# Where the gate rows of a two-mixer transformer step are computed, and in which order its first loads go out

## Chip, core and metric

One NeuronCore of a Trainium2 chip runs the whole program. The time is device microseconds (us) of one execution. An execution taken by the hardware profiler has two times: the time of that execution, and its span, from the first to the last instruction of the profile.

## What is computed

One inference step of a layer with two groups of heads, all in float32. 128 context tokens and 512 latent tokens (five token tiles of 128) have 2048 features each. Cut to what matters here:

```
mod                = silu(cond) @ w_ada + b_ada       # 2 conditionings (latent, context), w_ada 2048 x 6144
shift, scale, gate = split(mod, 3)                    # each 2 rows of 2048
h  = rms_norm(x, g_norm) * (1 + scale) + shift
z  = h @ w_in                                         # mixer A: 8 heads; mixer B: 8 heads, 2 KV heads
oa = differential attention of mixer A (softmax 1 - lambda * softmax 2), RMS norm, times silu(ga)
ob = grouped-query attention of mixer B with RMS norm on q and k, times silu(gb)
y  = rms_norm(x + gate * (concat(oa, ob) @ w_out), g_final)
```

Shift and scale are needed before any token is projected. The gate rows are needed only at the end, when the output projection is added to x. The keys and values of the context tokens are outputs too.

## The kernel before

**Passes.** The projections run as 17 passes (`ITS`) of 16 steps (`KT`, one per 128 features of the contraction). Every step multiplies five token tiles by one 128x512 block of weights into the PSUM tile `z_ps`. Each factor is split into a high and a low float32r part, so a tile costs three matmuls of 512 columns (L542, L543, L544), 15 in a step. Pass 0 (`KV_IT`) makes the keys and values of mixer B, passes 1 to 4 (`G_IT`) two query heads of mixer B each with their gates, passes 5 to 12 (`D_IT` to `OUT_IT - 1`) one head of mixer A each, and passes 13 to 16 the output projection, 512 columns each.

**Attention beside the projection.** While pass `it` is projected, TensorE does the attention of the group of pass `it - 1` between the token tiles, by the table `STEPS`: O (output rows of the group before) in step 1, QK (transposes of q and k) in step 3, then S (scores), T (transposes of the probabilities) and V (times the values) of tile after tile, with T of the last tile in step 14 and V of the last tile, called V4 below, in step 15, after the second token tile. ScalarE and VectorE each run one hand-ordered list per step: the split of the weights three steps ahead (`split_w`: ScalarE copies `w_raw` to `w_hi` at L794, VectorE subtracts at L1100), the evictions, maxima (L1180), exponentials, the subtraction of the softmaxes (L1197), the split of the transposed probabilities (`pt_los`, L1205), `v_lo`, `qk_los` (L1171), norms and rotary positions (`rotate`, L1129 to L1143). GpSimd takes reciprocal roots (`o_root`), the products with the gates (`gate_mul`) and a queue of DMAs of its own (`load_kv`, `state`, `spill`, `load_row`, `load_out_operands`). All other loads are on SyncE's queue. The three banks of `ring` (PSUM) are handed out by `count_turns`; a bank is claimed again when its last reader has freed it.

**Pass 0 and the start.** The shift and scale columns of w_ada (32 MB) come in 32 loads `load_ada(n)` of 1 MB (two DMAs of 512 KB) into a ring of five (`ADA_RING`). Each is one quarter of a block of two feature tiles, multiplied by the two conditioning columns (`modulation`, L562, 32 matmul instructions with two stationary columns). Four quarters are a block; VectorE takes its rows from PSUM (L1052), TensorE transposes them (`columns`, L575), and only then can two more feature tiles of h be scaled (`modulate`, L815 and L819) and split (`split_h`, L1092 and L1094). The work on block c+1 and c+2 stands between the token tiles of pass 0; the last quarter, (7, 3), is in step 12. SyncE issues four w_ada loads, the five tiles of x (1 MB each), load 4, the first two pairs of weight steps (`load_w`), and then the rest. ScalarE squares each x tile (L804), GpSimd takes the root, VectorE scales it (L1074), TensorE transposes it (L585). GpSimd's queue begins with the small tables: four broadcasts of 256 KB for lambda, three of 64 KB for norm weights, and the two rotary tables. VectorE uses the lambda tables in step 3 of pass 0 (`minus_lambda`).

**Gate rows.** The gate columns of w_ada (16 MB) come in 32 loads of 512 KB (`load_gate`, L494) on SyncE's queue into eight buffers that lie in attention tiles not yet used. TensorE multiplies them by the two conditioning columns (`step_gate`, L744) after 18 steps: 13, 14 and 15 of pass 0 and 0 to 14 of pass 1, one or two loads each, always into bank 0 of the ring. A load is two products of 128x2 stationary and 128x512 moving, whose outputs go to partitions 0, 32, 64 or 96, each of which runs as two matmul instructions. `gate_rows_out` (L1260, four additions on VectorE) adds the bias at the start of pass 2, and `norm_sums` and `gate_exp` of pass 1's group wait for the last gate product, since their tiles overlay the buffers. GpSimd loads the bias in pass 1 and writes the rows to DRAM in pass 2.

```
    take("GATE", [0])                                             # L170
            if it == G_IT + 1 and s == 0: gate_rows_out()         # L1363
STEPS = { 1: O, 3: QK, 4: S0, 5: S1, 6: T0, 7: S2 V0, 8: T1, 9: S3 V1, 10: T2, 11: S4 V2, 12: T3, 13: V3, 14: T4, 15: V4 }
```

## Time and profile before

| | |
|---|---|
| median of 3 runs | 1334.58 us (1333.96 to 1335.18) |
| the profiled execution | 1334.56 us |
| its span | 1332.8 us |
| TensorE busy | 1277.5 us, 96% of the span |
| VectorE, ScalarE, GpSimd busy | 719.2, 606.9, 216.7 us |
| DMA | 156.59 MB, mean 117 GB/s; 301 to 359 GB/s in the first four fortieths of the span |
| granted TensorE clock | 0.998 of full speed |

Busy times are of instructions on an engine. Matmuls are pipelined, so a row's duration is longer than the distance between two starts; where a length of TensorE work is wanted, starts are to be compared. A DMA's time to landing counts from its issue.

### The profile page before, as it was taken

What the parts mean: (1) busy time and instruction counts of PE and PEld (TensorE: products, weight loads), DVE (VectorE), ACT (ScalarE), POOL (GpSimd) and SP (SyncE); (2) the same over time, 40 slices, a digit from 0 to 9 for tenths busy, and PEclk for the clock granted to TensorE, in tenths of its full rate; (3) what the DMA queues carried; (4) which work ended last, traced back from release to release, by engine and by line L of the source; (5) the groups of instructions that cost most, each with busy time, mean ns of one, the idle gap of its engine ahead of it and who ended that gap; (6) DMA issues with size and microseconds to landing.
All of it is one profiled execution on the core that took longest, in us unless ns stands there. A gap on an engine that the chain in (4) does not pass through costs nothing.

```text
span 1332.8 us, 19103 instructions
## 1 busy us (share of the span) xinstructions
PE 1277.5 (96%) x7399; PEld 1009.7 (76%) x7399; DVE 719.2 (54%) x1155; ACT 606.9 (46%) x1297; POOL 216.7 (16%) x374
## 2 busy tenths in 40 slices
PE   2699999999999999999999999999999999999996
PEld 1466666788888888877778787878788787888885
DVE  1443531856647566465565656565656766523343
ACT  1322312454555545545554645555555665422123
POOL 2000110301103011021212222121213222200001
PEclk9999999999999999999999999999999999999999
DMA  9999784211212112131222121221213431433234
GB/s 301 359 353 347 273 275 142 64 48 48 69 47 83 48 48 76 52 92 48 82 65 77 59 78 56 68 81 49 85 48 108 124 107 64 138 132 134 79 135 158
DMA packets 144218, 156.59 MB, mean 117 GB/s; under 512 B 8008, under 2 KB 122792, under 8 KB 143360
## 3 DMA queue, kind: packets, MB, share of 16 engines
q1 hardware_dynamic: 137232, 132.19, 30.7%
q0 software_dynamic: 6896, 23.17, 5.3%
q8 instruction: 59, 0.97, 0.3%
q14 instruction: 31, 0.25, 0.1%
HBM read 144.18 MB, written 11.16 MB: 117 GB/s over the span
## 4 chain that ended last, share of the span: by engine, by line
PE 89%; DVE 3%; DMA 3%; SPq 2%; ACT 1%; issue 1%; POOL 0%; ACTq 0%; DVEq 0%
PE z_ps L542 24%; PE z_ps L544 22%; PE z_ps L543 22%; PE ring L637 5%; PE ring L718 5%; PE ring L673 4%; PE ring L720 2%; PE ring L562 2%; SPq L455 1%; DMA x_sb<-in_x_sample_dram 1%; PE ring L744 1%; PE ring L544 1%; PE ring L543 1%; PE ring L542 1%; DMA ada_raw<-in_w_ada_dram 1%; DMA w_raw<-in_w_in_dram 1%
## 5 line engine op out<-in xcount | busy, mean ns | idle before, releaser
L542 PE MATMUL z_ps<-w_hi,xt_hi 128*128 128x512 f32 x1360 | 570.6, 420 | 2.4 <-DVE xt_lo L1244 1.0
L544 PE MATMUL z_ps<-w_hi,xt_lo 128*128 128x512 f32 x1360 | 532.7, 392 | 0.0
L543 PE MATMUL z_ps<-w_lo,xt_hi 128*128 128x512 f32 x1360 | 532.1, 391 | 0.0
L1100 DVE TENSOR_TENSOR w_lo<-w_raw,w_hi 128x512 fp32r<-128x512 f32 x272 | 191.6, 707 | 247.7 <-ACT w_hi L794 245.7
L794 ACT ACTIVATE w_hi<-w_raw 128x512 fp32r<-128x512 f32 x272 | 170.4, 628 | 334.0 <-PE z_ps L544 321.6
L542 PEld LDWEIGHTS z_ps<-w_hi,xt_hi 128*128 128x128 f32 x1360 | 256.1, 188 | 80.5 <-issue 35.5
L544 PEld LDWEIGHTS z_ps<-w_hi,xt_lo 128*128 128x128 f32 x1360 | 255.6, 188 | 56.7
L543 PEld LDWEIGHTS z_ps<-w_lo,xt_hi 128*128 128x128 f32 x1360 | 257.3, 189 | 36.2
L1180 DVE TENSOR_REDUCE small<-s_sb 128x2 f32<-128x1536 f32 (+1 forms) x60 | 88.3, 1472 | 29.2 <-ACT s_sb L794 29.2
L896 ACT ACTIVATE s_sb<-s_sb,small 128x768 f32<-128x768 f32 (+1 forms) x120 | 97.9, 819 | 2.8 <-DVE small L1180 2.8
L718 PE MATMUL ring<-v_hl,pt_hi 128*128 128x256 f32 x400 | 96.2, 324 | 0.0
L794 ACT ACTIVATE o_sum<-ring 128x128 f32<-128x128 f32 (+1 forms) x60 | 18.8, 313 | 159.9 <-PE ring L720 159.9
L720 PE MATMUL ring<-v_hl,pt_lo 128*128 128x128 f32 x400 | 89.0, 223 | 0.0
L1205 DVE TENSOR_TENSOR pt_lo<-ring,pt_hi 128x256 fp32r<-128x256 f32 (+2 forms) x144 | 75.2, 527 | 24.4 <-ACT pt_hi L794 21.4
L794 ACT ACTIVATE pt_hi<-ring 128x256 fp32r<-128x256 f32 (+2 forms) x144 | 66.7, 467 | 47.0 <-PE ring L637 45.9
L1448 POOL TENSOR_TENSOR sg<-sg,zs 128x128 f32<-128x128 f32 (+1 forms) x60 | 37.0, 616 | 290.8 <-DVE sg L1163 290.1
L720 PEld LDWEIGHTS ring<-v_hl,pt_lo 128*128 128x128 f32 x400 | 76.3, 191 | 3.1
L718 PEld LDWEIGHTS ring<-v_hl,pt_hi 128*128 128x128 f32 x400 | 75.2, 188 | 3.2
L1163 DVE RECIPROCAL sg<-sg 128x128 f32<-128x128 f32 (+1 forms) x60 | 72.6, 1209 | 3.4 <-POOL sg L1442 3.4
L794 ACT ACTIVATE s_sb<-ring 128x512 f32<-128x512 f32 (+2 forms) x144 | 59.4, 464 | 29.0 <-PE ring L673 28.2
L637 PE MATMUL ring<-ident,s_sb 128*128 128x128 f32 x400 | 66.4, 272 | 0.0
L1216 DVE TENSOR_TENSOR o_sum<-ring,o_sum 128x128 f32<-128x128 f32 (+1 forms) x60 | 20.0, 334 | 84.8 <-ACT o_sum L794 84.8
(147 smaller groups left out, 1199.4 us busy)
## 6 DMA issues: line engine op xcount, KB each, us to landing
w_raw<-in_w_in_dram SPq DMA_DIRECT2D x208, 256.0 KB, 3.2
ada_raw<-in_w_ada_dram SPq DMA_DIRECT2D x64, 512.0 KB, 8.8
w_raw<-in_w_out_dram SPq DMA_DIRECT2D x64, 256.0 KB, 3.4
gate_pt<-in_w_ada_dram SPq DMA_DIRECT2D x12, 512.0 KB, 6.2
gate_sg<-in_w_ada_dram SPq DMA_DIRECT2D x12, 512.0 KB, 5.4
o_spill<-row_st POOLq DMA_DIRECT2D x14, 320.0 KB, 3.5
row_st<-o_spill POOLq DMA_DIRECT2D x14, 320.0 KB, 3.4
x_sb<-in_x_sample_dram SPq DMA_DIRECT2D x4, 1024.0 KB, 13.7
```

Source lines behind the costliest of these rows:

```text
L542: pe.matmul(out, hi_l, hi_r, start=start, stop=False)
L543: pe.matmul(out, hi_l, lo_r, start=False, stop=False)
L544: return pe.matmul(out, lo_l, hi_r, start=False, stop=stop)
L637: return pe.transpose(bank[:, col:col + P], src, ident[:, :])
L718: pe.matmul(bank[:, o:o + 2 * DH], pt_hi[:, c_, keys], v_hl[:, vh, vt, :], start=(j == 0), stop=False, skip_group_check=True)
L720: ins = pe.matmul(bank[:, o:o + DH], pt_lo[:, c_, keys], v_hl[:, vh, vt, 0:DH], start=False, stop=(j == tiles[-1][0]), skip_group_check=True)
L794: return act.activation(out, in_, ACT.Copy, **kw)
L896: act.activation(row, row, ACT.Exp, bias=nmax[:, t, c_:c_ + 1], accum_out=den[:, t, c_:c_ + 1]).then_inc(exp_done, 1)
L1100: dve.tensor_tensor(w_lo[:, b, :], w_raw[:, kg // 2 % RAW_RING, kg % 2, :], w_hi[:, b, :].bitcast(F32), ALU.subtract).then_inc(w_lo_done, 1)
L1163: dve.reciprocal(sg[:, t, 0:w], sg[:, t, 0:w]).then_inc(g_inv, 1)
L1180: dve.tensor_reduce(nmax[:, t, :], s_sb[:, t % 2, :, 0:(NKEY if t else P)], AX_X, ALU.max, negate=True).then_inc(max_ready, 1)
L1205: ins = dve.tensor_tensor(pt_lo[:, c_, keys], RB(n)[:, col:col + P * w], pt_hi[:, c_, keys].bitcast(F32), ALU.subtract)
```

## The change

- The gate rows are no longer 128 matmul instructions on TensorE in passes 0 and 1. VectorE sums them: for each of the 32 loads two pieces of 512 columns, and for each piece and conditioning one instruction, `acc = raw * weight + acc` with a weight per partition (for the first contraction tile a product alone). That makes 64 pieces of two instructions, 128 in all. `GATE_STEPS` puts twelve pieces into a pass, at the end of VectorE's list of steps 1 (two), 2, 3, 4, 9, 11, 13 (two), 14 and 15 (two), from step 4 of pass 6 to step 13 of pass 11.
- The sum over the 128 partitions is left to TensorE: one `step_gate` after step 0 of pass 12, with eight products of a 128x2 selector and the accumulators. Its bank is the third from the current one. `gate_rows_out` moves to step 1 of pass 12, the bias loads to pass 5, the store of the rows to step 3 of pass 12.
- The loads of the gate columns move from SyncE's to GpSimd's queue, two buffers of 512 KB, each loaded again when its second piece is summed.
- The attention tiles `q_hi` ... `pt_lo` are split by head into two halves; mixer A uses the first half alone, and the gate buffers and accumulators lie in the second. Their other uses change only in how they are indexed.
- At the start SyncE issues the five x tiles ahead of the w_ada loads, and `load_w(0)` ahead of load 4. TensorE does the first four transposes of x ahead of the first modulation block, VectorE the scaling of x ahead of taking its rows.
- GpSimd issues the lambda tables when six feature tiles of h are split, and the norm and rotary tables when twelve are. Their first uses on VectorE and ScalarE move to step 8 and step 15 of pass 0.

The re-indexing of the attention tiles is left out below, and so are the declarations of semaphores.

```diff
-GATE_SLOT = KT - 3
-GATE_END = 2 * KT - 1
-GATE_RING = 8
+GATE_COLS = D_MODEL // 2
+GATE_LOADS = 2 * KT
+GATE_STEPS = [1, 1, 2, 3, 4, 9, 11, 13, 13, 14, 15, 15]
+GATE_FROM = 4
+GATE_SUM_IT = OUT_IT - 1
...
-def gate_pieces(s):
-
-    def begin(s):
-        return min(max(0, 2 * KT * (s - GATE_SLOT) // (GATE_END - GATE_SLOT)), 2 * KT)
-    return range(begin(s), begin(s + 1))
+def gate_parts():
+
+    out, i = {}, 0
+    for it in range(D_IT + 1, GATE_SUM_IT):
+        for s in GATE_STEPS:
+            if i < 2 * GATE_LOADS and (it, s) >= (D_IT + 1, GATE_FROM):
+                out.setdefault((it, s), []).append(i)
+                i += 1
+    return out
+
+
+GATE_PARTS = gate_parts()
 
...
-    take("GATE", [0])
     b = 0
     for it in range(ITS):
         for s in range(KT):
+            if (it, s) == (GATE_SUM_IT, 0):
+                take("GATE", [(b + 2) % RING])
...
+    e = r1
+    q_hi, q_lo, k_hi, k_lo, v_hl, pt_hi, pt_lo = ([] for _ in range(7))
+    for i in range(2):
+        half0 = e
+        for name, tiles, shape in (("q_hi", q_hi, [P, TILES * P]), ("q_lo", q_lo, [P, TILES * P]),
+                                   ("k_hi", k_hi, [P, NKEY + P]), ("k_lo", k_lo, [P, NKEY + P]),
+                                   ("v_hl", v_hl, [P, 7, 2 * DH]), ("pt_hi", pt_hi, [P, NKEY]),
+                                   ("pt_lo", pt_lo, [P, NKEY])):
+            if (name, i) == ("pt_hi", 0):
+                pt0 = e
+            tile, e = place(f"{name}{i}", shape, F32R, e)
+            tiles.append(tile)
     assert e <= r1 + 4 * 12800
-    gate_q, _ = place("gate_q", [P, 2, D_MODEL // 2], F32, r1)
-    gate_pt, _ = place("gate_pt", [P, 3, D_MODEL // 2], F32, pt0)
+    gate_raw, e = place("gate_raw", [P, 2, GATE_COLS], F32, half0)
+    gate_acc, e = place("gate_acc", [P, 2, D_MODEL], F32, e)
+    gate_sel, e = place("gate_sel", [P, 2, 2], F32, e)
...
-            def load_gate(m):
-                if m >= GATE_RING:
-                    sp.wait_ge(gate_used, m - GATE_RING + 1)
-                elif m == 0:
-
-                    wait_full(sp, TURN[("ADA", BLOCKS - 1)])
-                elif m == 5:
-
-                    for u in range(2):
-                        wait_full(sp, TURN[("HT", KT - 1)] + u)
-                k, u = divmod(m, 2)
-                c0 = 2 * D_MODEL + u * (D_MODEL // 2)
-                sp.dma_start(gate_raw[m % GATE_RING], ada_v[k, :, c0:c0 + D_MODEL // 2]
-                             ).then_inc(gate_in[m % GATE_RING], 16)
-
-            for n in range(4):
-                load_ada(n)
             for t in range(TILES):
                 src = x_prompt[0] if t == 0 else xs_v[:, t - 1, :]
                 sp.dma_start(x_sb[:, t, :], src).then_inc(x_in[t], 16)
+            for n in range(4):
+                load_ada(n)
+            load_w(0)
             load_ada(4)
-            load_w(0)
             load_w(1)
 
             for n in range(ADA_RING, 4 * BLOCKS):
                 load_ada(n)
                 if n % 4 == 0 and n // 4 >= 2:
                     load_w(n // 4)
-            gates = 0
             for j in range(BLOCKS, ITS * KT // 2):
                 load_w(j)
-
-                room = 5 if j == BLOCKS else GATE_RING + gate_pieces(2 * j - 5).stop
-                while gates < min(room, 2 * KT):
-                    load_gate(gates)
-                    gates += 1
...
 
-            def step_gate(s):
+            def step_gate():
+
                 n = TURN["GATE"]
-                bank = claim(n) if s == GATE_SLOT else RB(n)
-                for m in gate_pieces(s):
-                    k, u = divmod(m, 2)
-                    pe.wait_ge(gate_in[m % GATE_RING], 16 * (m // GATE_RING + 1))
-                    for jj in range(2):
-                        j = 2 * u + jj
-                        ins = pe.matmul(bank[32 * j:32 * j + 2, :], csv[:, k, :],
-                                        gate_raw[m % GATE_RING][:, 512 * jj:512 * (jj + 1)],
-                                        start=(k == 0), stop=(k == KT - 1))
-                    if m < 2 * KT - 1:
-                        ins.then_inc(gate_used, 1)
-                    else:
-                        filled(ins, n)
-
+                bank = claim(n)
+                pe.wait_ge(sel_set, 4)
+                pe.wait_ge(gate_summed, 2 * GATE_LOADS)
+                for r in range(2):
+                    for j in range(4):
+                        ins = pe.matmul(bank[32 * j:32 * j + 2, :], gate_sel[:, r, :],
+                                        gate_acc[:, r, NCOL * j:NCOL * (j + 1)], start=(r == 0), stop=(r == 1))
+                filled(ins, n)
+
+            h_transpose(0, 0)
             for quarter in range(4):
                 modulation(0, quarter)
             columns(0)
-            h_transpose(0, 0)
             h_transpose(0, 1)
             modulation(1, 0)
 
...
                                 step_o(a, part)
                     project(it, s, between)
-                    if GATE_SLOT <= KT * it + s < GATE_END:
-                        step_gate(KT * it + s)
+                    if (it, s) == (GATE_SUM_IT, 0):
+                        step_gate()
 
             for t in range(TILES):
...
                 act.wait_ge(og_ready, before(OG_DONE, a))
-                if a == G_IT:
-
-                    wait_full(act, TURN["GATE"])
...
                         modulate(s + 1)
-                    if it == 0 and s == 3:
...
 
-            modulation_rows(0)
-            modulation_columns(0)
-
             for t in range(TILES):
                 dve.wait_ge(x_rstd, t + 1)
                 dve.tensor_scalar(x_sb[:, t, :], x_sb[:, t, :], stat[:, 1, t:t + 1], None, ALU.mult).then_inc(x_hat, 1)
+
+            modulation_rows(0)
+            modulation_columns(0)
 
             def minus_lambda():
 
...
                 link(dve.tensor_scalar(lam[:, 1, :], lam[:, 0, :], -LAM_INIT, None, ALU.add))
+
+            def weigh_norm():
+
...
                 dve.wait_ge(z_free, TILES * (a + 1))
-                if a == G_IT:
-
-                    wait_full(dve, TURN["GATE"])
...
                                          ALU.mult, ALU.mult).then_inc(y_right, 1)
+
+            def gate_sums(i):
+
+                m, piece = divmod(i, 2)
+                k, u = divmod(m, 2)
+                dve.wait_ge(gate_in[u], 16 * (k + 1))
+                if k:
+                    dve.wait_ge(gate_summed, i - 3)
+                raw = gate_raw[:, u, NCOL * piece:NCOL * (piece + 1)]
+                c0 = GATE_COLS * u + NCOL * piece
+                for r in range(2):
+                    acc, weight = gate_acc[:, r, c0:c0 + NCOL], cs[:, KT * r + k:KT * r + k + 1]
+                    if k == 0:
+                        ins = dve.tensor_scalar(acc, raw, weight, None, ALU.mult)
+                    else:
+                        ins = dve.scalar_tensor_tensor(acc, raw, weight, acc, ALU.mult, ALU.add)
+                ins.then_inc(gate_summed, 1)
 
...
                             modulation_columns(s // 2 + 1)
-                    if it == 0 and s == 3:
+                    if it == 0 and s == KT // 2:
                         minus_lambda()
+                    if it == 0 and s == KT - 1:
+                        weigh_norm()
                     old, late = late, steps_at(it, s)
...
                                 gated(a, t)
-                    if it == G_IT + 1 and s == 0:
+                    if (it, s) == (GATE_SUM_IT, 1):
                         gate_rows_out()
+                    for i in GATE_PARTS.get((it, s), []):
+                        gate_sums(i)
...
                                pattern=[[-1, P]], channel_multiplier=1).then_inc(id_set, 1)
+            def inv_root(out, in_, n, mean_of):
+
+                link(pool.tensor_scalar(out, in_, 1.0 / mean_of, EPS, ALU.mult, ALU.add))
+                return pool.tensor_tensor(out, out, half[:, 0:n], ALU.pow)
+
+            for t in range(TILES):
+                pool.wait_ge(x_sq, t + 1)
+                inv_root(stat[:, 1, t:t + 1], stat[:, 0, t:t + 1], 1, D_MODEL).then_inc(x_rstd, 1)
+
+            pool.wait_ge(h_lo, KT // 2 - 2)
             for i, v_ in enumerate((lam_q1, lam_q2, lam_k1, lam_k2)):
                 pool.dma_start(lam_raw[:, i, :], v_.rearrange("a h d -> a (h d)").broadcast_to([P, H_A * DK_A])
                                ).then_inc(lam_in, 16)
+            pool.wait_ge(h_lo, KT - 4)
             for i, v_ in enumerate((subln_g, q_norm_g, k_norm_g)):
                 pool.dma_start(norms[:, i, :], v_.broadcast_to([P, DH])).then_inc(norm_in, 16)
             pool.dma_start(rope_a[:, :, :, :], ropes_a).then_inc(rope_in, 16)
             pool.dma_start(rope_b[:, :, :, :], ropes_b).then_inc(rope_in, 16)
-
-            def inv_root(out, in_, n, mean_of):
-
-                link(pool.tensor_scalar(out, in_, 1.0 / mean_of, EPS, ALU.mult, ALU.add))
-                return pool.tensor_tensor(out, out, half[:, 0:n], ALU.pow)
-
-            for t in range(TILES):
-                pool.wait_ge(x_sq, t + 1)
-                inv_root(stat[:, 1, t:t + 1], stat[:, 0, t:t + 1], 1, D_MODEL).then_inc(x_rstd, 1)
 
             def load_kv(a):
 
...
 
+            def load_gate(m):
+
+                k, u = divmod(m, 2)
+                c0 = 2 * D_MODEL + GATE_COLS * u
+                pool.dma_start(gate_raw[:, u, :], ada_v[k, :, c0:c0 + GATE_COLS]).then_inc(gate_in[u], 16)
+
+            def gate_begin():
+
+                pool.wait_ge(og_ready, OG_DONE[D_IT - 1])
+                for m in range(2):
+                    load_gate(m)
+                for r in range(2):
+                    pool.memset(gate_sel[:, r, r:r + 1], 1.0).then_inc(sel_set, 1)
+                    pool.memset(gate_sel[:, r, 1 - r:2 - r], 0.0).then_inc(sel_set, 1)
+
             load_kv(0)
             late = []
...
                         load_row(s - (ROW_LAG - 1))
-                    if it == G_IT and s == 4:
-
-                        pool.wait_ge(qk_ready, G_IT)
+                    if (it, s) == (D_IT, 4):
+
                         for j in range(4):
                             for r in range(2):
                                 c0 = 2 * D_MODEL + 512 * j
                                 pool.dma_start(ada_rows[32 * j + r:32 * j + r + 1, :], b_ada[:, c0:c0 + 512]
                                                ).then_inc(gate_bias, 16)
...
                     late = [step for step in late if step[0] != "V" or step[2] < TILES - 1]
+                    if (it, s) == (D_IT + 1, 2):
+                        gate_begin()
+                    for i in past:
+                        if i % 2 and i // 2 + 2 < GATE_LOADS:
+                            pool.wait_ge(gate_summed, i + 1)
+                            load_gate(i // 2 + 2)
+                    past = GATE_PARTS.get((it, s), [])
```

## Rows read from the trace of the kernel before

**Rows 1.** The page's busy times and instructions of each engine
```profile
PE 1277.5 (96%) x7399; PEld 1009.7 (76%) x7399; DVE 719.2 (54%) x1155; ACT 606.9 (46%) x1297; POOL 216.7 (16%) x374
```

**Rows 2.** Waits of TensorE: who waited for whom, us in total, times, longest
```profile
PE ring L562 <- DMA ada_raw<-in_w_ada_dram: 16.0, 5, 12.2
...
PE ring L637 <- DVE ada_rows L1260: 0.8, 1, 0.8
...
PE ring L542 <- DVE q_lo L1171: 0.4, 1, 0.4
```

**Rows 3.** Windows: stretch, busy us (instructions) by engine, clock, DMA share, GB/s
```profile
101.00:115.00 14.00, 13.50 (x172) 9.55 (x171) 5.57 (x13) 3.88 (x7) 0.00 (x0) 1.00 1.10 354
...
228.00:250.00 22.00, 20.85 (x100) 16.82 (x99) 15.84 (x23) 9.59 (x17) 4.95 (x3) 1.00 0.17 52
250.00:316.00 66.00, 66.00 (x376) 56.68 (x375) 37.97 (x57) 36.12 (x76) 7.85 (x10) 1.00 0.15 48
```

**Rows 4.** Last w_ada DMAs, issued 122.6 to 124.6 us: issue ns, time to landing
```profile
L455 SPq DMA_DIRECT2D ada_raw<-in_w_ada_dram x2: 1417/1672/1927, 122.6 to 124.6; - x2
DMA to landing us min/median/max: 8.8/8.8/8.9
```

**Rows 5.** Timeline, end of pass 0: start, us, engine, line, operation, idle before
```profile
136.57 0.40 PE L562 MATMUL ring<-ada_raw,cs 128*2 128x128 f32 x7
...
145.54 0.83 DVE L1094 TENSOR_TENSOR xt_lo<-row_st,xt_hi 128x640 fp32r<-128x640 f32 x1
145.74 0.60 PE L744 MATMUL ring<-gate_q,cs 128*2 128x512 f32 x2
```

**Rows 6.** DMA queues in 0 to 16 us: packets, MB, share of 16 engines
```profile
q0 software_dynamic: 539, 1.63, 43.6%
```

**Rows 7.** Timeline at the start: last x tile squared, first projection matmul
```profile
38.20 1.88 ACT L804 ACTIVATE z_ps<-x_sb 128x2048 f32<-128x2048 f32 x1 [0.50 <-DMA x_sb<-in_x_sample_dram]
...
46.98 0.79 PE L542 MATMUL z_ps<-w_hi,xt_hi 128*128 128x512 f32 x1 [0.79 <-DVE w_lo L1100]
```

**Rows 8.** Timeline of TensorE: gate products after steps 15 and 0, and the last
```profile
155.53 1.04 PE L744 MATMUL ring<-gate_pt,cs 128*2 128x512 f32 x8
...
160.12 1.04 PE L744 MATMUL ring<-gate_sg,cs 128*2 128x512 f32 x8
...
226.59 1.04 PE L744 MATMUL ring<-gate_sg,cs 128*2 128x512 f32 x8
```

**Rows 9.** Timeline of TensorE: four token tiles of step 0 of pass 10
```profile
861.38 0.39 PE L542 MATMUL z_ps<-w_hi,xt_hi 128*128 128x512 f32 x1
...
864.11 0.60 PE L637 MATMUL ring<-ident,og 128*128 128x128 f32 x4
```

**Rows 10.** Timeline, steps 2 and 3 of pass 1: rotary end, QK transposes
```profile
169.17 0.69 DVE L1143 TENSOR_TENSOR zs<-rope_t 128x512 f32<-128x512 f32 x1
...
171.10 0.60 PE L637 MATMUL ring<-ident,zs 128*128 128x128 f32 x4
...
173.87 0.44 PE L637 MATMUL ring<-ident,kv_raw 128*128 128x128 f32 x2 [0.34 <-DVE k_lo L1171]
```

**Rows 11.** Groups of VectorE by form: count | busy us, mean ns | idle before
```profile
L1100 DVE TENSOR_TENSOR w_lo<-w_raw,w_hi 128x512 fp32r<-128x512 f32 x272 | 191.6, 707 | 247.7 <-ACT w_hi L794 245.7 <-DVE norms L1086 0.2
...
L1197 DVE SCALAR_TENSOR_TENSOR s_sb<-s_sb,small 128x768 f32<-128x768 f32 x32 | 32.6, 1019 | 1.1
...
L1287 DVE SCALAR_TENSOR_TENSOR y_sb<-y_sb,stat,gf_b 128x512 f32<-128x512 f32 x5 | 3.7, 746 | 1.1 <-POOL stat L1567 1.1
```

**Rows 12.** Timeline: steps 13 to 15 of pass 9, steps 3 and 4 of pass 10
```profile
851.60 0.29 DVE L1216 TENSOR_TENSOR o_sum<-ring,o_sum 128x128 f32<-128x128 f32 x1 [1.66 <-ACT o_sum L794]
...
853.04 1.12 DVE L1205 TENSOR_TENSOR pt_lo<-ring,pt_hi 128x512 fp32r<-128x512 f32 x2 [0.23 <-ACT pt_hi L794]
...
856.56 0.28 PE L718 MATMUL ring<-v_hl,pt_hi 128*128 128x256 f32 x1
...
875.58 0.28 DVE L1171 TENSOR_TENSOR q_lo<-ring,q_hi 128x128 fp32r<-128x128 f32 x1
...
876.38 0.33 PE L673 MATMUL ring<-k_hi,q_hi 64*128 64x128 f32 x2
```

**Rows 13.** DMAs of GpSimd's queue: issuing engine, count, KB each, us to landing
```profile
o_spill<-row_st POOLq DMA_DIRECT2D x14, 320.0 KB, 3.5
...
gf_b<-in_g_final_dram POOLq DMA_DIRECT2D x1, 1024.0 KB, 5.0
```

80 lines of the change are left out of this document (37 added, 43 removed).

## The prediction

> **What bounds the kernel now.** I read the busy times first: TensorE 96% of the span, VectorE 54% [rows 1]. Then its waits: what it loses to others is small after the first 47 us (the 16.0 us on w_ada loads are in all but 0.2 us the start) [rows 2]. The windows by stage show two regimes [rows 3]. From pass 1 on TensorE is full (66.00 of 66.00 us) and DMA nearly idle (48 GB/s). In pass 0 TensorE has 13.50 of 14.00 us, and the 16 DMA engines are full too, at 354 GB/s (the share reads 1.10). So every TensorE instruction removed after pass 0 is worth its length, unless a chain on VectorE was hidden under it; in pass 0 nothing is won that DMA does not deliver sooner. The sum is made against the profiled execution, 1334.56 us (span 1332.8 and 1.8 around it), which is the median shown within 0.02 us.
>
> **Pass 0: what the new order at the start is worth.** The x tiles go first and the tables late. The last x tile lands about 38.2, and the first projection is 8.8 us later [rows 7]. Of what must land before it, the tables go: GpSimd's queue took 43.6% of the 16 engines in the first 16 us, 7.0 us [rows 6]. The order of x and the first four w_ada loads changes what is last (w_ada, whose rows, transpose, scaling and split take a similar time), not the sum, so pass 0 starts some 7 us sooner, at about 40. But the tables are only moved: they are loaded in steps 5 to 11 of pass 0, where DMA is full, and cost their 7 us there, ahead of the last w_ada load. That load was issued at 124.6 and landed 8.8 us later, at 133.4 [rows 4], and TensorE used it at 136.57 [rows 5]. DMA work up to it is the same bytes, so it lands at 133.4 again and TensorE now waits for it: the gain at this point is the 3.1 us by which TensorE lagged. Bounds: 0, and 7.0 where the late tables find room. I take 3.1, since the DMA share leaves no room [rows 3].
>
> The gate loads leave SyncE's queue, where weights for pass 1 stood behind them; those come sooner, which nobody waits for, as `split_w` runs three steps ahead.
>
> **Gate products removed.** A gate product stands after 18 steps, from 145.74 to the last at 226.59 [rows 5, 8]. From 155.53 to 160.12 is one step of pass 1 with one such group, 4.59 us [rows 8]. Without one, four token tiles take 864.11 - 861.38 = 2.73, a step 3.41 [rows 9]. A group costs 1.18 us, whether it holds one load or two.
> - After steps 13 and 14 of pass 0: the next step needs the split of h, which ends at 145.54 + 0.83 = 146.37, 0.63 after the group's start at 145.74 [rows 5]; of 1.18 some 0.25 is left over after waiting, twice: 0.5.
> - After step 15 of pass 0 and steps 0, 1, 2 of pass 1 (4 groups, 4.7 us): nothing. Here the cover goes. The chain of mixer B's keys on VectorE ends at 169.17 + 0.69 = 169.86, its transposes started at 171.10, and the third of them already waited for `k_lo`, at 173.87 [rows 10]. The chain hangs on the end of pass 0, not on TensorE. TensorE now gets to QK 4.7 us sooner, waits about 3.5 us for the rotary product and the rest for `k_lo`, and passes this point as late as before.
> - After steps 3 to 14 of pass 1: 12 groups, each its full 1.18, 14.1 us. The steps there hold no other pieces, as those of rows 9, which run without a wait.
> - Pass 2: `gate_rows_out` leaves VectorE's list. The waits behind it, 0.8 and 0.4 [rows 2], and TensorE's 22.00 - 20.85 = 1.15 of idle there [rows 3]: 1.15, as the next passes have none. Bound below: 0.
>
> **Added on TensorE.** Eight products after step 0 of pass 12. The group of rows 8 has four products in its eight instructions, to four groups of partitions side by side, in 1.04. Two such rounds, one per accumulator, less the overlap, and one more start: 2.1. Bounds 1.2 and 4.7 (each product by itself at half of 1.18). `gate_rows_out` is then in step 1, ahead of QK, in the place of the two pieces of the other passes: nothing.
>
> **Added on VectorE: 128 instructions.** The same form with both inputs in SBUF is L1287, 746 ns; L1197 is 1019 ns for 768 columns [rows 11]. I take 0.67 from start to start, an estimate that lets one overlap the next by some 0.08 (bound: 0.746): 86 us in 5.5 passes, for an engine that is 54% busy [rows 1]. It fits; what counts is what is queued behind a piece in the list. `split_w` is three steps ahead. There are two tight places.
> - Step 13 holds two pieces. `o_high` ends at 851.60 + 0.29 = 851.89, four instructions end at 854.57, then `split_w` 0.6, then the 1.12 us of `pt_los` of the last tile, which started at 853.04: it ends at 856.3. V4 of TensorE starts at 856.56 [rows 12]. 0.2 us are left, which any further delay uses up.
> - Steps 1 to 3: three pieces stand ahead of `qk_los`, 4.0 us in idle places; the last `q_lo` is done at 875.86 and the first score product starts at 876.38 [rows 12]. By the same count it ends about as before, with 0.5 us to spare.
>
> **Added on GpSimd.** 32 loads of 512 KB. Between 320 KB in 3.5 and 1 MB in 5.0 us [rows 13] one takes about 4. The tightest is the load for the two pieces of step 15: its buffer is free after the first piece of step 13, at 853.2; GpSimd first does the root of V3, so it lands at 857.5 to 860, where VectorE wants it at 859. Up to 1 us of wait, with V4's `gated` and the rotary product of step 0 behind it. They have more than that; with it the margin of steps 1 to 3 is gone.
>
> Together I count 0.4 us per mixer A pass, in five passes with a full list: 2.0. Bounds 0 and 6 (the four instructions of step 13 at L1197's 1.02: 1.2 per pass). The bias loads in pass 5 and the store in pass 12 have no one behind them within a step: nothing.
>
> A word on a rule against this change. The rows show 512 columns from two SBUF inputs in 0.746 us and 768 in 1.019 [rows 11], about the pace of L1100's subtraction. The Trainium skill (Vector Engine (DVE) Microarchitecture Reference, section 7) says that this instruction form runs at half throughput with two SBUF sources that aren't bf16. The rows show no halving against L1100; by the rule each of the 128 would take some 1.2 us instead.
>
> **Sum.** -3.1 - 0.5 - 14.1 - 1.15 + 2.1 + 2.0 = -14.75: **1319.8 us**.
>
> **Rivals.**
> 1. *The start keeps its gain.* The late tables find room, and pass 0 ends 7.0 sooner instead of 3.1: 1315.9. For: first projection 7 us sooner. Against: DMA share 1.10 to the end. 0.12.
> 2. *VectorE's lists are late in every mixer A pass* by 1.2 more than counted, at V4 or at the first scores: 1326. For: margins of 0.2 and 0.5 us. 0.17.
> 3. *The groups covered other waits in pass 1 too* (weights, evictions), and the 14.1 become idle: 1334, no change. Against: passes 2 and 3 are full without them [rows 3]. 0.04.
> 4. *Slower: the sums themselves are slow.* At 1.22 us each (twice what L1100's 707 ns leave after the overlap) `pt_los` is late for V4 by four times 0.55 less 0.2, 2.0, and the scores by six times 0.55 less 0.5, 2.8: 4.8 per pass, in 5.5 passes 26 against 2.0 counted, so 1344. It decides from about 1.05 us each on. Against: both rows of this form. The rule above would make it so. 0.06.
> 5. *It doesn't do what it says*, in that work removed turns into idle time: for the first four groups this is in the forecast, for the rest it is rival 3.
>
> **Chances.** Forecast 0.61, the others as given. What a measurement of this kernel tells from no change is 0.2%, 2.7 us. Faster 0.90, same 0.04, slower 0.06. The range takes rivals 1 and 2, with the unknown of the eight products on top: 1314 to 1327.
>
> **What would show it.** First projection near 40 us; new waits of TensorE on w_ada loads inside pass 0, 4 us or so in all, and its last use at 133.5; if that is at 130, rival 1. A wait of about 3.5 us at L637 on the rotary product in pass 1, and from step 3 on steps of 3.41. Sums of 0.75 us on VectorE; waits of L718 or L720 on `pt_lo` and of L673 on `q_lo` or `k_lo` below 0.5 us per pass; if they are above 2, rival 2 or 4. Mixer A passes longer than before by no more than 0.5 us. The forecast is wrong if pass 1 is not 14 us shorter from step 3 on.

## The result and the profile after

| | before | changed |
|---|---|---|
| median of four runs each | 1334.38 us | 1327.21 us (1326.16 to 1329.63) |
| ratio, 95% interval | | 0.9948 (0.9931 to 0.9965) |
| the profiled execution, its span | 1334.56, 1332.8 us | 1326.4, 1324.6 us |

The change is faster by 7.2 us, half of the 14.8 forecast, and 0.2 us above the range. First the page after: busy times and the queues.

```profile
PE 1261.0 (95%) x7287; PEld 1009.7 (76%) x7287; DVE 795.4 (60%) x1283; ACT 607.6 (46%) x1297; POOL 245.6 (19%) x410
...
q1 hardware_dynamic: 132624, 115.42, 27.4%
q0 software_dynamic: 11504, 39.95, 9.6%
```

TensorE has 112 instructions fewer and 16.5 us less to do, VectorE 76 us more [rows 1]. The span fell by 8.2, so TensorE stands idle for about 8 us more than before. Its waits say where.

```profile
PE ring L579 <- DVE x_sb L1058: 16.3, 4, 10.3
PE ring L556 <- DMA ada_raw<-in_w_ada_dram: 10.8, 9, 4.4
...
PE ring L631 <- DVE zs L1130: 3.8, 1, 3.8
PE ring L667 <- issue: 3.7, 5, 0.7
PE ring L631 <- DVE og L1220: 2.3, 5, 0.7
```

Beside the start there are new waits of two kinds: one of 3.8 us on the rotary product of the keys, in pass 1, and two that come five times each, 6.0 us together. The first ends at 167.91. In the windows (same columns as [rows 3]) it reaches into 166 to 172; the others lie in 620 to 990 us, the passes of mixer A with sums:

```profile
82.00:96.00 14.00, 9.61 (x95) 6.49 (x92) 3.16 (x7) 2.07 (x4) 0.00 (x0) 0.80 1.01 300
101.00:115.00 14.00, 13.49 (x193) 9.62 (x185) 7.23 (x14) 2.50 (x7) 0.00 (x0) 1.00 1.10 354
166.00:172.00 6.00, 3.81 (x15) 2.71 (x16) 5.93 (x11) 1.20 (x2) 0.00 (x0) 0.74 0.34 108
228.00:250.00 22.00, 22.00 (x112) 18.41 (x111) 16.42 (x19) 12.33 (x29) 7.74 (x6) 1.00 0.23 70
620.00:990.00 370.00, 363.99 (x1904) 285.97 (x1904) 286.61 (x472) 193.47 (x454) 105.21 (x180) 1.00 0.36 107
```

The kernel before has no idle time in the last of them:

```profile
620.00:990.00 370.00, 370.00 (x1950) 293.04 (x1949) 220.35 (x362) 196.46 (x462) 80.36 (x155) 1.00 0.23 67
```

The passes can be timed by their first projection matmul, which the timeline of TensorE gives for each. All pass lengths below are distances of two such starts, in us:

| | before | changed | difference | forecast |
|---|---|---|---|---|
| first projection | 46.98 | 37.82 | -9.2 | about -7 |
| pass 1 starts | 156.50 | 153.04 | -3.5 | -4.8 (3.6, and 1.2 for the group after step 15) |
| pass 1 | 74.59 | 61.94 | -12.7 | -12.9 (14.1 less, of which the chain of the keys takes that group's 1.2 back) |
| pass 2 | 83.89 | 82.26 | -1.6 | -1.15 |
| passes 3 to 6 | 324.65 | 324.65 | 0 | 0 |
| passes 7 to 11 | 5 x 73.46 | 74.65, 75.20, 75.16, 74.99, 74.92 | **+7.6** | +2.0 |
| pass 12 | 75.05 | 77.14 | +2.1 | +2.1 |
| rest | | | -0.2 | 0 |

**What happens in passes 7 to 11.** The timeline of the changed kernel, steps 13 of pass 9 to 4 of pass 10:

```profile
838.71 2.73 DVE L1291 SCALAR_TENSOR_TENSOR gate_acc<-gate_raw,cs,gate_acc 128x512 f32<-128x512 f32 x4
...
841.08 1.01 POOL L1397 TENSOR_SCALAR small<-small 128x1 f32<-128x1 f32 x1 [5.28 <-ACT sq_o L908]
...
842.80 0.19 POOL L1469 TENSOR_TENSOR small<-small 128x1 f32<-128x1 f32 x1
...
843.02 0.63 POOL L1511 DMA_DIRECT2D gate_raw<-in_w_ada_dram  x1
...
847.99 2.74 DVE L1291 SCALAR_TENSOR_TENSOR gate_acc<-gate_raw,cs,gate_acc 128x512 f32<-128x512 f32 x4 [2.33 <-DMA gate_raw<-in_w_ada_dram]
...
851.65 0.66 PE L631 MATMUL ring<-ident,og 128*128 128x128 f32 x4 [0.49 <-DVE og L1220]
...
864.28 0.28 DVE L1158 TENSOR_TENSOR q_lo<-ring,q_hi 128x128 fp32r<-128x128 f32 x1
...
864.77 0.33 PE L667 MATMUL ring<-k_hi,q_hi 64*128 64x128 f32 x2 [0.73 <-issue]
```

The first piece of step 13 ends after two of the four sums that start at 838.71, about 840.1. From then on the buffer is free. But the root of V3 stands first in GpSimd's list. GpSimd, idle for 5.28 us, gets ScalarE's square for it at 841.08, 1.0 us after the buffer is free, works on it for 1.9 and issues the load at 843.02, 2.9 us late. The load lands at 847.95, 4.93 after its issue, and VectorE has waited 2.33 for it. Behind the sums of step 15 in VectorE's list stands `gated` of V4 (`og`), for which TensorE waits 0.49 in step 1, and then the rotary product, `qk_los` and the scores, which wait 0.73 in step 4. The split `q_lo` that the scores want ends at 864.56, so what the row calls issue is taken to be that.

### The profile page after: what moved, and what is told of

Its sections match the earlier page's. It is cut to its first block, busy times and chain, and to the rows that moved or that the text cites. A ratio compares the mean times of both kernels' runs of the same rounds, so it can differ in the third digit from the quotient of the medians.

```text
span 1324.6 us, 19068 instructions
## 1 busy us (share of the span) xinstructions
PE 1261.0 (95%) x7287; PEld 1009.7 (76%) x7287; DVE 795.4 (60%) x1283; ACT 607.6 (46%) x1297; POOL 245.6 (19%) x410
## 4 chain that ended last, share of the span: by engine, by line
PE 85%; DMA 4%; SPq 4%; DVE 3%; ACT 1%; issue 1%; POOL 1%; ACTq 0%; DVEq 0%
PE z_ps L536 23%; PE z_ps L538 21%; PE z_ps L537 21%; PE ring L631 5%; PE ring L712 5%; PE ring L667 4%; SPq L470 3%; DMA gate_raw<-in_w_ada_dram 2%; DMA ada_raw<-in_w_ada_dram 2%; PE ring L714 2%; PE ring L556 1%; PE ring L538 1%; PE ring L537 1%; PE ring L536 1%; DVE gate_acc L1291 1%
## 5 line engine op out<-in xcount | busy, mean ns | idle before, releaser
L1291 DVE SCALAR_TENSOR_TENSOR gate_acc<-gate_raw,cs,gate_acc 128x512 f32<-128x512 f32 x120 | 85.1, 759 | 11.5 <-DMA gate_raw<-in_w_ada_dram 11.5
```

Source lines behind the costliest of these rows:

```text
L1291: ins = dve.scalar_tensor_tensor(acc, raw, weight, acc, ALU.mult, ALU.add)
```

## The experiments

All ratios are to the kernel before on the same chip.

### 1 and 2: the load for step 15, or the sums?

Only the first two gate loads are made, so the 128 sums run on the data of these two:

```diff
-                dve.wait_ge(gate_in[u], 16 * (k + 1))
+                dve.wait_ge(gate_in[u], 16)
...
                     for i in past:
-                        if i % 2 and i // 2 + 2 < GATE_LOADS:
-                            pool.wait_ge(gate_summed, i + 1)
-                            load_gate(i // 2 + 2)
+                        pass
```

> The changed kernel, but only the first two of the 32 gate loads are made and VectorE sums those two buffers again and again, so no sum waits for a load (the gate rows then hold wrong sums; all 128 instructions stay). Passes 7 to 11 took 74.65 to 75.20 us in the changed kernel against 73.46 before, 7.6 us in all. Theory L (the load for the two pieces of step 15 comes late, the list of VectorE stands for 2.3 us and the first scores and the output rows are late after it): passes of 73.5 to 73.7, the whole some 6.5 to 7.5 us faster than the changed kernel, about 1319.5. Theory S (the 2.7 us of sums ahead of the splits are too much for the list by themselves): passes stay at 74.6 to 75.2 and the time at 1326 to 1327.

Measured: 1318.62 us, 0.9881 (0.9866 to 0.9896), passes 7 to 11 at 73.46 (one at 73.60). The window:

```profile
620.00:990.00 370.00, 370.00 (x1943) 292.66 (x1942) 290.93 (x477) 198.18 (x466) 92.60 (x160) 1.00 0.22 67
```

VectorE does all the sums (290.93 us busy in 370, against 220.35 before) and TensorE never waits. So the sums by themselves cost nothing, and what the five passes lost (they take 7.5 us less here than in the changed kernel) hangs on the loads. The second run keeps every load and only moves its issue ahead of the root:

```diff
+                    for i in past:
+                        if i % 2 and i // 2 + 2 < GATE_LOADS:
+                            pool.wait_ge(gate_summed, i + 1)
+                            load_gate(i // 2 + 2)
+                    past = GATE_PARTS.get((it, s), [])
                     for kind, a, t in late:
                         if kind == "V":
                             o_root(a, t)
```

(and the same lines go from behind it.)

> The changed kernel with GpSimd's list turned round: in each step the reload of a gate buffer stands ahead of the roots for the fourth and fifth token tile. The load for step 15 was issued at 843.0 behind the root of V3, though its buffer was free at 840.1, landed at 847.9 and was wanted at 845.65. Theory L: issued at about 840.2 it lands at 844.7 to 845.2, the wait of 2.3 us goes, passes 7 to 11 take 73.5 to 74.0, the whole is 5 to 7 us faster than the changed kernel, about 1320.5. If the roots behind a load are then late for VectorE, some of it comes back at `gated` (0.6 us a pass). Theory S: no change.

Measured: 1318.64 us, 0.9879 (0.9863 to 0.9896). GpSimd's timeline, the same load in pass 9:

```profile
835.87 0.64 POOL L1511 DMA_DIRECT2D gate_raw<-in_w_ada_dram  x1 [4.62 <-DVE gate_acc L1291]
836.58 0.96 POOL L1397 TENSOR_SCALAR small<-small 128x1 f32<-128x1 f32 x1
```

The issue comes 0.3 us after the piece is summed (835.57), ahead of the root. The load lands at 840.04 and the sums of step 15 start at 841.03. VectorE waits for no load and TensorE for nothing: the same time as with no loads at all. The order of two items on GpSimd's queue was worth 7.5 us in passes 7 to 11 (367.43 instead of 374.93); the medians, taken in two comparisons, differ by 8.6.

### 3: smaller pieces in the loads

Four buffers of 256 KB instead of two of 512, each reloaded when its one piece is summed; the order on GpSimd stays as in the change.

```diff
-    gate_raw, e = place("gate_raw", [P, 2, GATE_COLS], F32, half0)
+    gate_raw, e = place("gate_raw", [P, 4, NCOL], F32, half0)
...
-                dve.wait_ge(gate_in[u], 16 * (k + 1))
+                dve.wait_ge(gate_in[i % 4], 16 * (k + 1))
...
-                raw = gate_raw[:, u, NCOL * piece:NCOL * (piece + 1)]
+                raw = gate_raw[:, i % 4, :]
...
-                        if i % 2 and i // 2 + 2 < GATE_LOADS:
+                        if i + 4 < 2 * GATE_LOADS:
                             pool.wait_ge(gate_summed, i + 1)
-                            load_gate(i // 2 + 2)
+                            load_gate(i + 4)
```

> The changed kernel with the same buffer space cut into four buffers of 512 columns instead of two of 1024: 64 loads of 256 KB, each issued when its own piece is summed, so every load has three other pieces between its issue and its use. Twice as many DMA issues of 0.6 us on GpSimd. Theory L: no wait for gate loads on VectorE, passes 7 to 11 of 73.5 to 73.8, 6 to 7.5 us faster than the changed kernel, about 1319.8. Theory S: no change. If GpSimd's issues are what costs, it gets slower than the changed kernel by some 1 us a pass.

Measured: 1320.39 us, 0.9892 (0.9877 to 0.9907). Two passes keep part of the wait (74.49 and 74.63 us long), three have none. VectorE's waits there:

```profile
DVE gate_acc L1291 <- DMA gate_raw<-in_w_ada_dram: 3.7, 2, 1.9
```

I had counted the distance of a load in pieces. The order on the queue is as before: in every pass the load of the second piece of step 15 still stands behind the root and goes out 2.9 us after its buffer is free. Three times it lands 3.9 to 4.5 us later, just in time (VectorE waits 0.14 us at most), and twice it takes 5.7 and 5.8, which are the two waits. Why it took longer there is open. A finer load shortens the landing and leaves no margin.

### 4: the new order at the start alone

The kernel before, with the x tiles first, the late tables and what goes with them (the parts of the change above from `for n in range(4)` on, and GpSimd's); the gate products stay on TensorE.

```diff
-            for n in range(4):
-                load_ada(n)
             for t in range(TILES):
...
+            for n in range(4):
+                load_ada(n)
+            load_w(0)
+            load_ada(4)
```

> The kernel before with the new start alone (x ahead of w_ada, first transposes ahead of the first block, tables after six and twelve feature tiles), gate products left on TensorE. In the changed kernel the last w_ada quarter is used at 134.63 instead of 136.57. Theory D (DMA full through pass 0, so moved tables cost there what they cost at the start): 1.9 us faster than before, 1332.6, and the first projection at 37.8. Rival: the start is worth its 9.2 us and the sums of the change eat the rest: 1326 to 1329.

Measured: 1332.73 us, 0.9984 (0.9975 to 0.9994); the first projection is at 37.80, pass 1 starts at 153.28, 3.2 us sooner. The interval lies within 0.2% of no change but for its lower edge. 9.2 us at the front become 3.2 at the end of pass 0, and 1.8 in the medians of this comparison, less than the profiled runs' 3.3 (1332.8 less 1329.5). The profiled run was the fastest of ten, 1.4 below their median, so the medians are the better measure; they agree with the 1.9 expected.

### 5: the tables early again

The changed kernel with the tables issued first, as before the change:

```diff
+            for i, v_ in enumerate((lam_q1, lam_q2, lam_k1, lam_k2)):
+                pool.dma_start(lam_raw[:, i, :], v_.rearrange("a h d -> a (h d)").broadcast_to([P, H_A * DK_A])
+                               ).then_inc(lam_in, 16)
...
-            pool.wait_ge(h_lo, KT // 2 - 2)
...
-            pool.wait_ge(h_lo, KT - 4)
```

> The changed kernel with all tables issued first on GpSimd's queue, as before; x still ahead of w_ada. Theory D (DMA is the clock of pass 0, bytes and their time are conserved): the first projection is later than 37.8 by some 6 to 7 us, pass 1 still starts at 153.0 within 1 us, and the time is that of the changed kernel, 1326 to 1327.5. Rival (late tables find room beside w_ada): pass 1 starts 3 us or more later, 1330.

Measured: 1328.27 us, 0.995 (0.9936 to 0.9963). The first projection comes at 45.20, 7.4 us later than in the changed kernel, and pass 1 starts at 153.11 against 153.04. So the late tables, taken alone, were worth nothing: their DMA time was moved within pass 0. The two kernels get to the same end by different limits. With early tables the last w_ada DMA lands at 132.90 and TensorE, running from 45.20, uses it 1.8 us later; with late ones it lands at 134.36 and is used 0.3 later.

### 6: the tables where DMA is idle

Experiment 2, with the norm and rotary tables after the last w_ada block (GpSimd waits for its product), the lambda tables in step 5 of pass 1 in two tiles of their own, their arithmetic in step 9:

```diff
-            pool.wait_ge(h_lo, KT // 2 - 2)
...
-            pool.wait_ge(h_lo, KT - 4)
+            wait_full(pool, TURN[("ADA", BLOCKS - 1)])
...
+                    if (it, s) == (1, 5):
+                        for i, v_ in enumerate((lam_q1, lam_q2, lam_k1, lam_k2)):
+                            dst = (lam_q if i < 2 else lam_k)[:, i % 2, :]
+                            pool.dma_start(dst, v_.rearrange("a h d -> a (h d)").broadcast_to([P, H_A * DK_A])
+                                           ).then_inc(lam_in, 16)
```

> As e2, with the tables out of pass 0's DMA stretch: norm and rotary tables wait until the last w_ada block is multiplied, the lambda tables are loaded in step 5 of pass 1 into the unused end of the score buffer and into the row buffer, and their arithmetic moves to step 9 of pass 1. Theory D: pass 0 sheds the 6 to 7 us that the tables take of a full DMA, the 4.4 us wait at 87 us and the half clock after it go, the last quarter is used at about 128 instead of 134.6, pass 1 starts at about 146.3, and the whole is 6 to 7 us faster than e2: 1312. Rival (TensorE bounds pass 0 by itself from 37.8 on): the last quarter is used at 133 or later, at most 2 us faster than e2.

Measured: 1312.78 us, 0.9834 (0.982 to 0.9847); pass 1 starts at 147.76, 5.3 us sooner than in the changed kernel and 5.0 sooner than in experiment 2. The last w_ada DMA lands at 126.94 against 134.35 in experiment 2: the 7.4 us that the same tables cost at the front in experiment 5. TensorE uses it 2.4 us after it has landed, so the rest of the 7.4 is not won. In the window of pass 0 where the lambda tables had been:

```profile
82.00:96.00 14.00, 13.50 (x182) 9.53 (x185) 5.57 (x13) 4.11 (x7) 0.00 (x0) 1.00 1.09 352
```

13.50 us of TensorE against 9.61 in the changed kernel, a clock of 1.00 against 0.80, 352 GB/s against 300.

### 7: a shorter chain for the keys

What is left in pass 1 is the wait of 3.8 us. Here the product of the keys with their norm weights goes ahead of the product with the roots, while GpSimd makes these, and `v_lo` goes to step 4:

```diff
                                 norm_reduce(it - 1)
+                                z2 = zs[:, :, 0:2 * DH].rearrange("p t (c d) -> p t c d", c=2)
+                                w = norms[:, 2, :]
+                                link(dve.tensor_tensor(z2, z2, w.unsqueeze(1).unsqueeze(1).broadcast_to(
+                                    [P, TILES, 2, DH]), ALU.mult))
...
-                        if s == 2:
+                        if s == (4 if it == 1 else 2):
                             v_lo(it - 1)
```

> As e6, with the chain of mixer B's keys on VectorE shortened in pass 1: the product with the norm weights (1.5 us) is made while GpSimd takes the roots, and the split of the values moves from step 2 to step 4. In the changed kernel TensorE waits 3.8 us for the rotary product at QK and then for k_lo. Theory C (this chain, not TensorE, sets the start of QK, which is why the first four gate groups bought nothing): the rotary product ends 1.5 us sooner, k_lo some 3.5 us sooner, pass 1 takes 58.3 to 59 instead of 61.9, and the whole is 3 to 3.6 us faster than e6, about 1308.6. Rival (the wait is for GpSimd's roots or for the eviction of z): below 1 us.

Measured: 1312.11 us, 0.983 (0.9816 to 0.9843), pass 1 at 61.37: 0.4 of the 3 us. GpSimd's timeline of this kernel, the roots of the keys:

```profile
153.07 1.37 POOL L1405 TENSOR_SCALAR stat<-stat 128x10 f32<-128x10 f32 x1 [8.21 <-DVE stat L1104]
154.52 2.41 POOL L1406 TENSOR_TENSOR stat<-stat,half 128x10 f32<-128x10 f32 x1
```

and VectorE's beside it:

```profile
152.88 1.48 DVE L1352 TENSOR_TENSOR zs<-zs,norms 128x1280 f32<-128x1280 f32 x1
154.40 0.69 DVE L1092 TENSOR_TENSOR w_lo<-w_raw,w_hi 128x512 fp32r<-128x512 f32 x1
156.97 1.49 DVE L1116 TENSOR_TENSOR zs<-zs,stat 128x1280 f32<-128x1280 f32 x1 [1.88 <-POOL stat L1406]
```

In experiment 6 the two were shorter, 0.57 and 1.99, and in the kernel before, where VectorE was idle beside them, 0.21 and 1.99 (last line):

```profile
152.90 0.57 POOL L1399 TENSOR_SCALAR stat<-stat 128x10 f32<-128x10 f32 x1 [8.20 <-DVE stat L1104]
153.56 1.99 POOL L1400 TENSOR_TENSOR stat<-stat,half 128x10 f32<-128x10 f32 x1
```

```profile
160.50 0.21 POOL L1397 TENSOR_SCALAR stat<-stat 128x10 f32<-128x10 f32 x1 [8.24 <-DVE stat L1115]
```

GpSimd's ten-element instruction ends at 154.44, 0.08 us after VectorE's product (154.36). In experiment 6 it was not alone either: it ended at 153.47, 0.07 after a VectorE subtraction of 0.68 us (`w_lo`, 152.72 to 153.40). From its start to the end of the roots it takes 3.86 us instead of 2.65, 1.2 more: the product that was to be free in the shadow of the roots held them up by most of its own 1.48 us. The Trainium skill has the rule (SBUF — State Buffer, section "Who interferes with whom"): a VectorE instruction with two SBUF inputs and a GpSimd instruction that reads SBUF exclude each other for the whole length of whichever is first. The trace agrees: both times VectorE's was first and GpSimd's ended 0.07 to 0.08 us behind it.

### 8 and 9: the keys' transposes two steps later

If the chain can't be made shorter, TensorE can do something else meanwhile. QK of mixer B's keys goes from step 3 to step 5 of pass 1, in the changed kernel (9) and in that of experiment 6 (8):

```diff
+KV_STEP = 5
...
-        if not 0 <= a < OUT_IT or (group_kind(a) == "KV" and kind != "QK"):
+        if not 0 <= a < OUT_IT or group_kind(a) == "KV":
             continue
         out.append((kind, a, t))
+    if (it, s) == (1, KV_STEP):
+        out.append(("QK", KV_IT, 0))
```

> The changed kernel with the same single move of QK from step 3 to step 5 in pass 1. By theory C the same 5.5 us are saved here, pass 1 falls from 61.9 to about 56.4 us and the time to about 1321.7; passes 7 to 11 keep their 74.6 to 75.2 us. By the rival less than 1 us, 1326.5.

Measured: 1322.05 us, 0.9913 (0.9896 to 0.993); pass 1 takes 57.05 us, 4.9 less than in the changed kernel (61.94), passes 7 to 11 stay at 74.6 to 75.4. Against the kernel before pass 1 has now lost 17.5 us, which is its 15 groups of gate products at 1.17 each: what the forecast took for lost behind the chain of the keys was to be had.

> The kernel of the late tables (1312.8 us) with one edit: in pass 1 the normed keys and their gate products for mixer B (QK) move from step 3 to step 5. Theory C, that pass 1's first 15 us are set by the chain from the gates to the transposed keys: gates and norm weights are ready about 14.4 us after the end of pass 0 and k_lo about 18.3 us after it, whichever step the work stands in, so TensorE, with two more projections in front of it, has no wait of 3 to 4 us, and the clock is not halved behind it. Pass 1 takes about 56.2 to 56.5 us in place of 61.7, the time comes to about 1307.3. Rival, that the evictions and loads of the new projections bound pass 1 and the wait only moves: less than 1 us, 1312.

Measured: 1314.37 us, 0.9846 (0.9831 to 0.986), no better than experiment 6. Pass 1 takes 63.12 us. ScalarE's timeline shows the wait in its new place:

```profile
160.18 0.63 ACT L789 ACTIVATE w_hi<-w_raw 128x512 fp32r<-128x512 f32 x1 [2.77 <-PE z_ps L543]
169.94 0.63 ACT L789 ACTIVATE w_hi<-w_raw 128x512 fp32r<-128x512 f32 x1 [9.12 <-DMA w_raw<-in_w_in_dram]
170.47 1.07 ACT L789 ACTIVATE k_hi<-ring 128x512 fp32r<-128x512 f32 x2
```

The eviction of the transposed keys stands in ScalarE's list behind the copy of a weight block that has not landed (issued at 162.17, 7.74 us to landing), and TensorE waits 5.5 us for `k_lo`. The DMA queues in 158 to 168 us of this run:

```profile
q0 software_dynamic: 415, 1.31, 69.0%
q1 hardware_dynamic: 319, 0.31, 9.7%
...
w_raw<-in_w_in_dram SPq DMA_DIRECT2D x4, 256.0 KB, 6.3
```

The four lambda loads went out at 158.6 to 160.8 us, just there. With them GpSimd's queue (q0) holds 69.0% of the engines; in the same stretch of experiment 12, without them, 7.5%, and the weight loads take 2.9 us.

### 10 to 12: the lambda loads once more

Experiment 8 with its lambda loads in GpSimd's step 9 and their arithmetic in step 13:

```diff
-                    if (it, s) == (1, 5):
+                    if (it, s) == (1, 9):
                         for i, v_ in enumerate((lam_q1, lam_q2, lam_k1, lam_k2)):
```

> The kernel before in this series (late tables, keys at step 5; 1314.4 us, with a wait of 5.5 us and ScalarE's 9.12 us for w_raw behind the four lambda loads of 158.6 to 160.8 us) with one edit: the lambda loads move from step 5 to step 9 of pass 1 and their arithmetic from step 9 to step 13. If those 1 MB of one-row loads beside the projection's weights are what took the gain back, the weights land in time, the wait goes, pass 1 falls from 63.1 to about 57 us as in the changed kernel with the keys at step 5 alone, and the time comes to about 1308. Rival: the weights are late again wherever the lambda loads stand, since each projection block needs 256 KB every 3.4 us; then the wait returns at step 9 to 11 and the time stays at 1312 to 1314.

Measured: 1313.71 us, 0.9846 (0.9832 to 0.9859), the same wait (5.2 us), because the loads were issued in the same place:

```profile
158.96 1.07 POOL L1574 DMA_DIRECT2D lam_q<-in_lam_q_dram  x2
160.02 1.06 POOL L1574 DMA_DIRECT2D lam_k<-in_lam_k_dram  x2
```

GpSimd has nothing to do in those steps of pass 1 and runs ahead of the others; a step in its list is no time. In the last two runs a wait holds it, one load per two steps or all four in step 9:

```diff
-                    if (it, s) == (1, 9):
-                        for i, v_ in enumerate((lam_q1, lam_q2, lam_k1, lam_k2)):
+                    if it == 1 and s in (7, 9, 11, 13):
+                        pool.wait_ge(w_lo_done, KT + s + 1)
+                        i = (s - 7) // 2
+                        for v_ in ((lam_q1, lam_q2, lam_k1, lam_k2)[i],):
```

> In the run before, the lambda loads kept their place (158.96 to 161.08 us on GpSimd, which runs ahead of the steps), so the edit changed nothing. Here each of the four loads first waits for the weights of its step to be split (steps 7, 9, 11, 13 of pass 1), so one of 256 KB goes out per two steps, and the arithmetic stands in step 15. If the burst beside the projection's weights took the gain back, the wait of 5.2 to 5.5 us for k_lo is gone, pass 1 takes 57 to 58 us instead of 63.3, and the time is about 1308. Rival, the weights come late by the same bytes wherever these stand: each load adds 1 to 1.5 us of wait on the weights, pass 1 takes 61 to 63 us and the time stays near 1313.

Measured: 1308.97 us, 0.9807 (0.9794 to 0.982), pass 1 at 58.63; the wait for `k_lo` is 0.8 us. A new one of 1.4 us is at the end of pass 1, where the exponential of lambda, waiting for VectorE in step 15, stands ahead of the evictions of `z_ps`.

```diff
                     if (it, s) == (1, 9):
+                        pool.wait_ge(w_lo_done, KT + s + 1)
```

> The four lambda loads together, held by the same wait until step 9 of pass 1, the arithmetic in step 13. If it is the coincidence with the transposed keys that costs (ScalarE's queue holds the weight's cast in front of the keys' eviction), pass 1 falls to 57 to 58 us, 1308, here too. If any burst of 1 MB starves the projection, TensorE waits 5 to 6 us for weights in steps 10 to 12 and the time is 1313 to 1314.

Measured: **1307.69 us**, 0.98 (0.9787 to 0.9814), pass 1 at 57.15, the fastest of all. ScalarE's timeline:

```profile
165.57 0.63 ACT L789 ACTIVATE w_hi<-w_raw 128x512 fp32r<-128x512 f32 x1 [4.52 <-DMA w_raw<-in_w_in_dram]
...
176.77 0.63 ACT L789 ACTIVATE w_hi<-w_raw 128x512 fp32r<-128x512 f32 x1 [2.77 <-PE z_ps L543]
181.04 0.63 ACT L789 ACTIVATE w_hi<-w_raw 128x512 fp32r<-128x512 f32 x1 [3.64 <-DMA w_raw<-in_w_in_dram]
```

The same four loads, issued at 171.6 to 173.7, make one copy 0.87 us late (3.64 against 2.77), which the lead of three steps swallows. So a burst of 1 MB alone doesn't starve the projection. At 165.57 the copy is 1.75 us late with no lambda load near it (4.52 against 2.77): there the burst of experiment 8 came on top of a lateness of its own, with the keys behind it. The trace shows where this one comes from. The load itself is quick, issued at 162.42 and landed 3.1 us later, but SyncE could not issue it sooner: its buffer was freed by VectorE's split, and that stood in VectorE's list behind the norm and rotary products of the keys.

```profile
160.68 0.69 DVE L1135 TENSOR_TENSOR zs<-rope_t 128x512 f32<-128x512 f32 x1
161.29 0.68 DVE L1095 TENSOR_TENSOR w_lo<-w_raw,w_hi 128x512 fp32r<-128x512 f32 x1
```

## Why the prediction was half right

**Start and pass 0: right in mechanism, 1.2 us too much.** Forecast was a conserved DMA time: earlier start, same end, and the gain is what TensorE lagged. Experiment 5 parts the 9.2 us at the front: 7.4 are the tables' (forecast 7.0), and 1.8 the order of x and w_ada, which the forecast put at nothing. Of the 7.4 only 0.1 is left at the end of pass 0, and experiment 6 finds them again as DMA time when the tables leave pass 0, so rival 1 is out. The last w_ada quarter was used at 134.63, not at 133.4 to 133.5. Its last DMA was issued at 122.8, 1.8 us sooner than before, and landed at 134.36, 0.9 later than forecast. The cause of the 0.9 is open. The lambda loads do slow what is beside them: in 84 to 94 us they take 39.5% of the DMA engines, the mean rate is 277 GB/s against 354 in the window of 101 to 115, and TensorE waits 4.39 us, which with 0.48 and 1.97 makes 6.8 us of waits on w_ada in pass 0, not 4. But the same start in experiments 1, 4, 3, 9 and 2 landed that DMA at 132.8, 133.3, 134.1, 134.2 and 134.4, so 0.9 us is no more than executions differ by.

**Groups in pass 1: right.** -14.1 forecast from the end of pass 0, -13.7 measured (12.65 in the pass and 1.06 ahead of it). The wait of about 3.5 us on the rotary product came as forecast, at 3.83, and the first four groups' 4.7 us went into it. The last sentence of the prediction asks for 14 us less from step 3 on. To the letter it is 9.1 from the start of step 3 (60.80 to 51.74), where the new wait now lies, and 12.9 from the first transpose of QK (59.99 to 47.07), behind which the clock is at half for 3.4 us. But I took the chain as a floor. It was one only for a QK in step 3: experiment 9 gets 4.9 us out by moving QK, and with it the whole 17.5.

**Pass 2** gave 1.6 instead of 1.15, **pass 12** cost 2.1 as forecast: the eight products are 1.90 us in sixteen instructions. That it is 2.1 to the tenth is luck: in the experiments with the same products pass 12 is 1.6 to 2.6 us longer than before.

```profile
1000.32 1.90 PE L738 MATMUL ring<-gate_acc,gate_sel 128*2 128x512 f32 x16
```

**Added on VectorE: right, and rival 4 is out.** By form, the 120 sums with an accumulator take (min/median/max ns):

```profile
L1291 DVE SCALAR_TENSOR_TENSOR gate_acc<-gate_raw,cs,gate_acc x120: 736/744/948, 614.5 to 989.3; 128x512 f32<-128x512 f32 x120
...
  DMA gate_raw<-in_w_ada_dram: 11.5, 5
```

Four take 2.73, 0.68 each (0.67 was forecast). No halving, and experiment 1 shows that the lists of VectorE hold them at no cost, less than the 0.4 us per pass I gave them and the GpSimd loads together. Both margins that I had counted, 0.2 and 0.5 us, were enough.

**The step that failed: "Added on GpSimd", where the load for step 15 was given "up to 1 us of wait", and 0.4 us per pass for all.** It was 2.3 us of wait and 1.2 to 1.7 us per pass, 7.6 instead of 2.0; with 2.0 in its place the change would have come to 1321. The mechanism, root first, load second, was named. The size was wrong in two ways.

The first is the load's way. Counted from the moment its buffer is free, the forecast had it land 4.3 to 6.8 us later (857.5 to 860 for 853.2) for a need 5.8 us later (859). It landed 7.9 later (847.95 for 840.1), for a need 5.5 later. The late end of the forecast, 1 us of wait, had the root end 2.8 after the buffer was free and gave the load 4. Measured were 2.9 and 4.93, and the need came 0.3 sooner: 1 + 0.1 + 0.9 + 0.3 = 2.3 us. So the load's own time is the larger part of the miss: the 32 gate loads took 4.4 us in the median, these five 4.9 to 5.1, as long as a 1 MB load in [rows 13]. And the late end was the case to count with. Of the 2.9 us, 1.0 is the wait for ScalarE and 1.9 the root, whose three instructions took 1.1 in the kernel before:

```profile
854.18 0.19 POOL L1397 TENSOR_SCALAR small<-small 128x1 f32<-128x1 f32 x1 [5.29 <-ACT sq_o L921]
```

In the changed kernel this instruction takes 1.01 us and ends at 842.09, 0.05 after the split `w_lo` of VectorE that follows the four sums (842.04), as in experiment 7. By this the sums held the root up without costing VectorE's list anything; no run parts this from the rest.

The second is what was queued behind, `gated` and the rotary product, to which I gave "more than that" without counting it: of 2.33 us 0.49 came through at the transposes of V4's output rows and 0.73 at the scores, where the margin was 0.5. These rows hold 6.0 of the 7.6 us (370.00 less 363.99 in the window); the other 1.6 have no wait of their own in the trace and stay open, though experiments 1 and 2 remove them too.

Rival 2 gave about this time, 1326, and what it says came true: VectorE's lists were late in passes 7 to 11, at the first scores and at the transposes of V4's output rows, by 1.1 us per pass more than counted (1.5 against 0.4). But it gave the narrow margins as the reason, and the sums alone did not use these up (experiments 1 and 2); the late load did.

The result is thus the forecast with one term at four times its size (+5.6), pass 0 short by 1.2 and pass 1 by 0.4, and pass 2 better by 0.5: 1319.8 + 5.6 + 1.2 + 0.4 - 0.5 = 1326.5, where the profiled execution has 1326.4. The median of the four runs, 1327.21, is 0.8 above it, and they spread over 3.5 us, so a tenth in this sum says little.
